# The first RMS norm of a two-model kernel: loads in pieces, squares on two engines, h in tiles of its own

## The reference, cut to what matters

```python
def _rmsnorm(x, g):
    xf = x.astype(jnp.float32)
    y = xf * lax.rsqrt(jnp.mean(xf * xf, axis=-1, keepdims=True) + EPS)
    return (y * g.astype(jnp.float32)).astype(x.dtype)

h = _rmsnorm(x, mix_norm_even[i])                 # x: 512 x 1024
cq, ckv, k_rope, rq, rk, rv, rg = _split(h @ w_in_even[i], EVEN_SPLIT)
...                                               # attention and retention, projection, FFN;
                                                  # then three more layers of other kinds
```

## Time and profile before

| | us |
|---|---|
| median of 3 runs | 2610.37 (2609.48 to 2611.45) |
| profiled execution, whole | 2610.0 |
| its span, first to last instruction | 2608.2 |
| mean granted TensorE clock | 0.948 of full |
| PE busy | 2327.7 (89%) |
| DVE busy / ACT busy / POOL busy | 1249.5 / 1218.0 / 251.7 |

### The profile page before, as it was taken

One profiled execution on the slowest core, in us unless ns is written; L12 is line 12 of the kernel. 1 busy time (PEld: TensorE's weight loads), 2 busy tenths in 40 slices (PEclk: granted clock), 3 DMA queues, 4 the chain that ended last, 5 costly groups with the idle time before them and its releaser, 6 DMA issues.

```text
span 2608.2 us, 29069 instructions
## 1 busy us (share of the span) xinstructions
PE 2327.7 (89%) x11390; PEld 1063.0 (41%) x11390; DVE 1249.5 (48%) x2431; ACT 1218.0 (47%) x2096; POOL 251.7 (10%) x332
## 2 busy tenths in 40 slices
PE   5989998999989888899989899979987899888994
PEld 1434653444434444344434346533323343343332
DVE  3556645456445435575564494543116544543213
ACT  5633555666547445555565664531116563321112
POOL 0000000000001220000000000112220201111131
PEclk8999999999999989999999999979998999888997
DMA  4220002221223200221222221439972220227996
GB/s 172 74 108 8 1 33 89 106 97 67 89 95 118 78 33 33 81 97 65 87 83 106 97 90 52 185 112 383 399 286 99 76 104 16 106 92 267 406 410 252
DMA packets 67753, 335.87 MB, mean 129 GB/s; under 512 B 12008, under 2 KB 12040, under 8 KB 53408
## 3 DMA queue, kind: packets, MB, share of 16 engines
q1 hardware_dynamic: 50448, 266.11, 26.9%
q0 software_dynamic: 17168, 67.90, 6.8%
HBM read 370.64 MB, written 23.07 MB: 151 GB/s over the span
## 4 chain that ended last, share of the span: by engine, by line
PE 64%; DVE 17%; ACT 11%; issue 5%; DMA 2%; POOL 1%; DVEq 0%; SPq 0%; ACTq 0%; POOLq 0%
PE PB L3007 8%; PE PB L375 7%; PE PB L376 7%; PE PB L377 7%; DVE WS L313 4%; PE PB L3031 4%; ACT junk L254 4%; PE PB L1548 2%; PE PB L1550 2%; PE PB L1549 2%; PE PB L2994 1%; PE PB L508 1%; ACT WS L300 1%; DMA T<-moe_x,small 1%; PE PB L789 1%
## 5 line engine op out<-in xcount | busy, mean ns | idle before, releaser
L375 PE MATMUL PB<-AS,WS 128*128 128x512 f16 x1480 | 569.6, 385 | 70.0 <-DVE AS L445 33.5
L376 PE MATMUL PB<-AS,WS 128*128 128x512 f16 x1480 | 569.4, 385 | 0.0
L377 PE MATMUL PB<-AS,WS 128*128 128x512 f16 x1480 | 568.4, 384 | 0.0
L313 DVE SCALAR_TENSOR_TENSOR WS<-raw,sc,WS 128x1024 f16<-128x1024 f32 (+3 forms) x288 | 327.0, 1196 | 103.5 <-ACT WS L300 103.5
L300 ACT ACTIVATE WS<-raw,sc 128x1024 f16<-128x1024 f32 (+3 forms) x288 | 283.9, 1056 | 40.8 <-DVE sc L280 40.8
L254 ACT ACTIVATE junk<-raw 128x1024 f16<-128x1024 f32 (+3 forms) x288 | 280.5, 974 | 8.9
L375 PEld LDWEIGHTS PB<-AS,WS 128*128 128x128 f16 x1480 | 146.0, 99 | 276.6 <-issue 65.2
L3007 PE MATMUL PB<-T 128*64 128x512 f32 x768 | 233.7, 613 | 14.3 <-issue 11.6
L377 PEld LDWEIGHTS PB<-AS,WS 128*128 128x128 f16 x1480 | 146.5, 99 | 180.3 <-issue 10.0
L376 PEld LDWEIGHTS PB<-AS,WS 128*128 128x128 f16 x1480 | 146.0, 99 | 175.6 <-issue 14.3
L289 DVE TENSOR_REDUCE sc<-sc 128x1 f32<-128x4 f32 x72 | 11.3, 157 | 364.0 <-POOL sc L268 364.0
(11 more groups left out here) (580 smaller groups left out, 3392.5 us busy)
## 6 DMA issues: line engine op xcount, KB each, us to landing
T<-in_moe_up SPq DMA_DIRECT2D x26, 2048.0 KB, 10.0
raw<-in_w_up SPq DMA_DIRECT2D x22, 2048.0 KB, 8.0
T<-in_moe_down SPq DMA_DIRECT2D x26, 1024.0 KB, 12.6
raw<-in_w_down SPq DMA_DIRECT2D x16, 1408.0 KB, 6.0
raw<-in_w_in_even SPq DMA_DIRECT2D x9, 2048.0 KB, 8.1
raw<-in_w_in_odd SPq DMA_DIRECT2D x8, 2048.0 KB, 7.8
moe_y<-X SPq DMA_DIRECT2D x32, 512.0 KB, 10.0
WS<-in_moe_up SPq DMA_DIRECT2D x6, 2048.0 KB, 14.7
```

Source lines behind the costliest of these rows:

```text
L313: e.scalar_tensor_tensor(lo[q], raw[q], s, hi[q], MUL, SUB).then_inc(*k.s("dve_split").up("lo", i, q))
L375: e.matmul(bank, wh[:, q, c, :], act.hi[c], start=c == 0, stop=False)
L376: e.matmul(bank, wh[:, q, c, :], act.lo[c], start=False, stop=False)
L377: m = e.matmul(bank, wl[:, q, c, :], act.hi[c], start=False, stop=c == kt - 1)
```

## The change

The loads are cut: `ones` alone, X in two halves, the four quarters of the first weight chunk, then csts without `ones` in two parts, each with a semaphore of its own. The engines no longer wait for all of X and csts at the start; PE waits for cols and `ones`, the others for cols, and what else a step reads is waited for at the step. ACT squares x tiles 0, 2, 4, 6 and DVE tiles 1, 3, 5, 7, into eight tiles of their own; DVE adds them in pairs, and PE sums four tiles in place of eight. The squares of the first weights lie around the reciprocal root, two quarters before and two after. h has eight tiles of its own, four of them are made before the scale of the weights is waited for, and the halves of h and those of the weights are written in an interleaved order. Finally `pe_tile` waits, in chunks of four tiles, for the quarter of its own tile, in all projections and not only in the first.

```diff
-    w.wait_ge(*k.s(f"raw{i % 2}").past(i))
+    w.wait_ge(*(k.s(f"raw{i % 2}").past(i) if i else k.s(f"first{q}").past("w")))
@@ pe_tile
-    w.wait_ge(*k.s("dve_split").past("lo", i, 3))
+    w.wait_ge(*k.s("dve_split").past("lo", i, q if CHUNKS[i][2] - CHUNKS[i][1] == 4 else 3))
@@ setup_sp
-    e.dma_start(k.X[:, :, :], k.ins["xT"].rearrange("(t p) s -> p t s", p=128)).then_inc(*k.s("in_x").dma("x"))
-    e.dma_start(k.csts[:, :], k.ins["csts"]).then_inc(*k.s("in_csts").dma("csts"))
-    sp_load(k, e, w, 0)
+    e.dma_start(k.cst("ones"), k.ins["csts"][:, ones:ones + 128]).then_inc(*k.s("in_ones").dma("ones"))
+    for j in range(2):
+        e.dma_start(k.X[:, 4 * j:4 * j + 4, :], k.ins["xT"][512 * j:512 * j + 512, :].rearrange("(t p) s -> p t s", p=128)).then_inc(
+            *k.s(f"x_half{j}").dma("x"))
+    for q in range(4):
+        e.dma_start(k.quarters(0)[1][q], k.ins[CHUNKS[0][0]][q].rearrange("p k c -> p (k c)")).then_inc(*k.s(f"first{q}").dma("w"))
+    e.dma_start(k.csts[:, 0:ones], k.ins["csts"][:, 0:ones]).then_inc(*k.s("in_csts").dma("left"))
+    e.dma_start(k.csts[:, ones + 128:], k.ins["csts"][:, ones + 128:]).then_inc(*k.s("in_csts").dma("both"))
     sp_load(k, e, w, 1)
@@ setup_act, setup_dve, setup_pool (setup_pe: in_ones in their place)
-    w.wait_ge(*k.s("in_x").past("x"))
-    w.wait_ge(*k.s("in_csts").past("csts"))
@@ even0_pe
-    stat(KT, 7, "norm")
+    for i in range(4):
+        w.wait_ge(*v.past("pair", i))
+        e.matmul(PB[7][:, :], k.cst("ones"), m.sq8[2 * i], start=i == 0, stop=i == 3).then_inc(*p.up("sum", "norm", i))
@@ even0_act
-    squares(k.x, m.tmp, "norm")
-    act_squares(k, e, w, 0)
-    w.wait_ge(*p.past("sum", "norm", KT - 1))
+    for i in range(0, KT, 2):
+        w.wait_ge(*k.s(f"x_half{i // 4}").past("x"))
+        e.activation(m.sq8[i], k.x[i], ACT.Square).then_inc(*a.up("square", "norm", i))
+    act_square(k, e, w, 0, 0)
+    act_square(k, e, w, 0, 1)
+    w.wait_ge(*p.past("sum", "norm", 3))
     act_rstd(k, e, w, m.tmp[2], PB[7][:, :], D, k.col("eps6"), "rstd", "norm", sig=a)
-    act_hi(k, e, w, 0)
-    act_norm(k, e, w, "even0", m.tmp)
+    act_square(k, e, w, 0, 2)
+    act_square(k, e, w, 0, 3)
+    normed(0)
+    normed(1)
+    act_hi_quarter(k, e, w, 0, 0)
+    normed(2)
+    normed(3)
+    act_hi_quarter(k, e, w, 0, 1)
+    for i in range(4, KT):
+        normed(i)
+    act_hi_quarter(k, e, w, 0, 2)
+    act_hi_quarter(k, e, w, 0, 3)
+    w.wait_ge(*k.s("in_csts").past("both"))
@@ even0_dve
+    for i in range(1, KT, 2):
+        w.wait_ge(*k.s(f"x_half{i // 4}").past("x"))
+        e.tensor_tensor(m.sq8[i], k.x[i], k.x[i], MUL).then_inc(*v.up("square", i))
+        w.wait_ge(*v.now())
+        w.wait_ge(*a.past("square", "norm", i - 1))
+        e.tensor_tensor(m.sq8[i - 1], m.sq8[i - 1], m.sq8[i], ADD).then_inc(*v.up("pair", i // 2))
+    dve_gains(k, e, w)
+    w.wait_ge(*a.past("rstd", "norm"))
+    for i in range(4):
+        normed(i)
     dve_scale(k, e, w, 0)
-    dve_lo(k, e, w, 0)
-    dve_norm(k, e, w, "even0", "mix_even", m.tmp)
+    normed_lo(0)
+    normed_lo(1)
+    dve_lo_quarter(k, e, w, 0, 0)
+    normed(4)
+    normed(5)
+    normed_lo(2)
+    normed_lo(3)
+    normed(6)
+    normed(7)
+    dve_lo_quarter(k, e, w, 0, 1)
+    for i in range(4, KT):
+        normed_lo(i)
+    dve_lo_quarter(k, e, w, 0, 2)
+    dve_lo_quarter(k, e, w, 0, 3)
```

More of the change, by code:

```diff
@@ L553, in setup_sp @@
 def setup_sp(k, e, w):
+    ones = CST["ones"][0]
     e.dma_start(k.cols[:, :], k.ins["cols"]).then_inc(*k.s("in_cols").dma("cols"))
-    e.dma_start(k.X[:, :, :], k.ins["xT"].rearrange("(t p) s -> p t s", p=128)).then_inc(*k.s("in_x").dma("x"))
-    e.dma_start(k.csts[:, :], k.ins["csts"]).then_inc(*k.s("in_csts").dma("csts"))
-    sp_load(k, e, w, 0)
+    e.dma_start(k.cst("ones"), k.ins["csts"][:, ones:ones + 128]).then_inc(*k.s("in_ones").dma("ones"))
[6 more added lines that the diff above has]
+    e.dma_start(k.csts[:, ones + 128:], k.ins["csts"][:, ones + 128:]).then_inc(*k.s("in_csts").dma("both"))
     sp_load(k, e, w, 1)
 def setup_act(k, e, w):
-    a = k.s("act_setup")
     e.preload_act_table_set(LN_EXP)
     w.wait_ge(*k.s("in_cols").past("cols"))
-    w.wait_ge(*k.s("in_x").past("x"))
-    w.wait_ge(*k.s("in_csts").past("csts"))
     for i, name in enumerate(("mix_even", "ffn0", "mix_odd", "ffn1")):
@@ L579, in setup_dve, with dve_gains @@
 def setup_dve(k, e, w):
-    v = k.s("dve_setup")
     w.wait_ge(*k.s("in_cols").past("cols"))
-    w.wait_ge(*k.s("in_x").past("x"))
-    w.wait_ge(*k.s("in_csts").past("csts"))
     ln = k.sc[:, 56:62].rearrange("p (a b) -> p a b", b=2)
     w.wait_ge(*k.s("act_junk").past("lnb", 2))
-    e.tensor_tensor(k.sc[:, 52:55], ln[:, :, 0], ln[:, :, 1], ADD).then_inc(*v.up("ln"))
+    e.tensor_tensor(k.sc[:, 52:55], ln[:, :, 0], ln[:, :, 1], ADD).then_inc(*k.s("dve_setup").up("ln"))
+def dve_gains(k, e, w):
     w.wait_ge(*k.s("pool_setup").past("gain"))
-    scale_of(e, w, v, k.sc[:, 56:63], 10, k.sc[:, 64:71], k.sc[:, 72:79], k.sc[:, 80:87], "gain")
+    scale_of(e, w, k.s("dve_setup"), k.sc[:, 56:63], 10, k.sc[:, 64:71], k.sc[:, 72:79], k.sc[:, 80:87], "gain")
 def setup_pool(k, e, w):
     w.wait_ge(*k.s("in_cols").past("cols"))
-    w.wait_ge(*k.s("in_x").past("x"))
-    w.wait_ge(*k.s("in_csts").past("csts"))
     w.wait_ge(*k.s("dve_setup").past("ln"))
@@ L601, in setup_pe @@
     w.wait_ge(*k.s("in_cols").past("cols"))
-    w.wait_ge(*k.s("in_x").past("x"))
-    w.wait_ge(*k.s("in_csts").past("csts"))
+    w.wait_ge(*k.s("in_ones").past("ones"))
 def even0_tiles(k):
@@ L609, in even0_tiles @@
         rq, rk, rv, rg = ([k.t(i) for i in range(a, a + 4)] for a in (0, 4, 8, 12))
+        sq8, h0 = [k.t(8 + i) for i in range(KT)], [k.t(i) for i in range(KT)]
         cq, kro, ckv = [k.t(i) for i in (16, 17, 18)], k.t(19), [k.t(20), k.t(21)]
@@ L875, in squares, with normed @@
             e.activation(tmp[i % 2], x, ACT.Square).then_inc(*a.up("square", what, i))
-    squares(k.x, m.tmp, "norm")
-    act_squares(k, e, w, 0)
-    w.wait_ge(*p.past("sum", "norm", KT - 1))
-    act_rstd(k, e, w, m.tmp[2], PB[7][:, :], D, k.col("eps6"), "rstd", "norm", sig=a)
-    act_hi(k, e, w, 0)
-    act_norm(k, e, w, "even0", m.tmp)
+    def normed(i):
+        w.wait_ge(*k.s("dve_setup").past("gain"))
+        w.wait_ge(*v.past("h", "norm", i))
+        e.activation(k.as_hi[i], m.h0[i], ACT.Identity, scale=k.sc[:, 64:65]).then_inc(*a.up("hi", "norm", i))
+    for i in range(0, KT, 2):
[4 more added lines that the diff above has]
+    w.wait_ge(*p.past("sum", "norm", 3))
+    act_rstd(k, e, w, m.tmp[2], PB[7][:, :], D, k.col("eps6"), "rstd", "norm", sig=a)
+    act_square(k, e, w, 0, 2)
[10 more added lines that the diff above has]
+    act_hi_quarter(k, e, w, 0, 3)
+    w.wait_ge(*k.s("in_csts").past("both"))
     for t in range(4):
@@ L1064, in even0_dve, with normed, normed_lo @@
     act = k.normed_parts("even0", 0)
-    dve_scale(k, e, w, 0)
-    dve_lo(k, e, w, 0)
-    dve_norm(k, e, w, "even0", "mix_even", m.tmp)
+    def normed(i):
+        e.scalar_tensor_tensor(m.h0[i], k.x[i], k.col("mix_even", i), m.tmp[2], MUL, MUL).then_inc(*v.up("h", "norm", i))
+    def normed_lo(i):
+        w.wait_ge(*v.past("h", "norm", i))
+        w.wait_ge(*a.past("hi", "norm", i))
+        e.scalar_tensor_tensor(k.as_lo[i], m.h0[i], k.sc[:, 64:65], k.as_hi[i], MUL, SUB).then_inc(*v.up("lo", "norm", i))
+    for i in range(1, KT, 2):
[8 more added lines that the diff above has]
+        normed(i)
+    dve_scale(k, e, w, 0)
+    normed_lo(0)
[12 more added lines that the diff above has]
+    dve_lo_quarter(k, e, w, 0, 3)
+    w.wait_ge(*k.s("in_csts").past("both"))
     for t in range(8):
```

## The result

| | before | after |
|---|---|---|
| median (runs measured side by side) | 2609.93 (2609.3 to 2611.45, 4) | 2592.51 (2586.87 to 2593.24, 4) |
| ratio, 95% interval | | 0.9928 [0.9911, 0.9945] |
| profiled execution, its span | 2610.0, 2608.2 | 2592.3, 2590.5 |
| mean granted TensorE clock | 0.948 | 0.949 |

The change takes 17.4 us off. The forecast was 2592.6. The total is right to 0.1 us, yet the trace shows only 15.1 of the 17.8 us of gain in the place where the prediction looked for them.

What follows compares the result with a forecast made beforehand. PE is the bound from 48.3, so the gain is its last k-tile of tile 0 starting at 30.4 in place of 48.26. Execution 2610.0 - 17.8 = 2592.2, median 0.4 above: 2592.6; range 2587 to 2598.5.

Steps and rivals of the forecast that it cites:

- half 0 of X lands: Loads at the start: 1.05 MB at 311 to 421 GB/s, 2.5 to 3.4 us before 10.2, plus 0.4: 7.9.
- last pair to the root's start: PE's sum of squares: ends 1.2 us after the last pair at 13.3, so the root starts at 14.5.
- ladder: scale to the last low half of h: DVE behind the weights' scale: 12 norm instructions at 0.70 and two weight quarters at 1.22, 10.8 us, from 19.6 to 30.4.
- tile 4 starts: First projection on PE: tiles 1 to 3 run from 31.1 to 46.6, then tile 4; the stage moves whole.
- rival 3: Loads at the start are served singly, not streamed; last k-tile at 49, total 2611, no change; chance 0.02.
- Rival 4: PE, let in earlier, drops to 1.2 GHz in loops that DVE bounds; two such chunks give 2627; chance 0.03.
- SP issues one load more ahead of it, some 0.4: Loads at the start: one more load issued ahead of half 0 of X delays its landing by some 0.4 us.
- a wait for a load after 11: Named sign that the forecast is wrong: ACT or DVE waiting for a load after 11 us.
- Rival 2: Smaller gain at the start, 11 to 14 us (late pieces, POOL's sum, clock, slower pairs): 2596 to 2600; chance 0.09.
- the central value: POOL's first sum of the gains: no cost taken, since it runs in X's shadow; 1.4 us kept for the range.
- later clock dips falling otherwise, +-1: Forecast's own spread: TensorE clock drops falling elsewhere move the total by +-1 us; runs differ by 2.0.
- rival 1: Finer waits pay in later chunks too: up to 10.4 us more, 2582.2; chance 0.06.

Runs made afterwards that it cites:

- the other kernels of the table: Variants of the changed kernel with edits to waits, ladder order, loads, squares, PE warming or `ones`, and the changed kernel rerun; medians 2588.14 to 2599.18.
- again: The changed kernel itself, unedited, measured once more beside the kernels with ones made on the chip: 2591.01, ratio to before 0.9932.
- ones made: The changed kernel with `ones` written by a DVE memset in place of a load: 2588.14, ratio to before 0.9925.
- the four kernels of the table above: Before (2609.93), changed (2592.51), changed measured again (2591.01), and changed with five extra float32 matmuls warming PE ahead of the sums (2590.21).

## Why the prediction was right, step by step

| step | forecast | measured | off by |
|---|---|---|---|
| half 0 of X lands | 7.9 | 9.2 | +1.3 |
| landing to the last pair | 5.4 | 5.7 | +0.3 |
| last pair to the root's start | 1.2 | 2.5 | +1.3 |
| root's start to the weights' high half | 5.1 | 5.4 | +0.3 |
| ladder: scale to the last low half of h | 10.8 | 10.3 | -0.5 |
| tile 4 starts | 46.6 | 49.4 | +2.8 |

**Right.** The mechanism: what the change is worth is the time by which the last k-tile of tile 0 comes sooner, and everything behind it moved with it. Of its 17.8 us it had 7.3 behind the scale of the weights, and 7.8 were measured there; the other 10.5 were to come from a sooner scale, and that gave 7.3. The ladder was right to 0.5, with 0.68 for each instruction of the norm (2.73 for four) in place of 0.70. The quarters held ACT up by no more than 0.1 (the first landed at 13.45, its square began at 13.48), hidden behind the sum; csts left the chain, and chunk 1 was ready in time. The squares on DVE take 0.69 each, as the nearest row said. The pieces were streamed and not served singly, so rival 3 is out: half 1 landed 3.0 behind half 0, 1.05 MB at some 350 GB/s, and the quarters 1.3 behind one another. The Trainium skill gives its two microseconds for each DMA (DMA: Bandwidth & Descriptors, section "Anatomy of one DMA — SWDGE (gpsimd) path") for loads issued from GpSimd, and no such price for each piece is seen in this queue of loads. (There are nine pieces in place of three loads, not eight.) Rival 4 did not happen: the mean granted clock is 0.949 against 0.948.

**Wrong in size: the landing.** The term "SP issues one load more ahead of it, some 0.4" was mis-sized: that load costs 1.6 to 2.7 us from profile to profile, and only 0.46 of it by its issue. Other terms of the step were too careful: without the small load in front the half lands at 6.5 to 7.0 where the step's arithmetic would give some 7.5. Half 1 was forecast for 10.4 and landed at 12.2, where ACT and DVE waited for it (1.82 and 0.22): one of the signs that the prediction itself had named for being wrong, a wait for a load after 11.

**Wrong in size: the sum.** "PE's last sum ended 1.2 after the last square" was read from a PE that had seven sums done. The change makes the sums start earlier and halves them, and so removes the work that warmed PE. The row from which the price was read had a condition that the change took away. Rival 2 named the start's clock only for the first tile. There it cost nothing: 1.2 GHz until about 30.3, where PE still waited for DVE (0.64 before 31.21).

**POOL.** DVE had the sum of the gains ready at 7.16 and POOL began at 9.68. In the other kernels of the table it began between 7.57 and 11.10. So the delay is real, but it stays hidden behind the root, as the central value had it.

**Why the total was right all the same.** At tile 4 the lead was 15.06, at the end 17.73. The lead over the kernel before (ACT's instructions matched one to one; the time is that of the kernel before, "fine in 0" has the finer waits in chunk 0 only, "no fine" has none):

```
at (us)     100    180    300    1000   1500   2300   2400   end
after      15.06  15.06  15.95  16.51  16.26  16.39  18.40  17.73
fine in 0  15.44  15.44  16.24  16.72  16.46  18.69  18.31  17.86
again      16.22  14.66  15.12  15.20  14.92  17.11  16.72  15.82
ones made  17.98  16.47  17.17  17.56  17.28  20.22  22.80  21.88
no fine     6.34   6.35   6.92   7.07   6.82   9.71  12.18  12.05
```

The two large steps of the first row come where PE runs at half clock in one kernel and not in the other. Before has such a stretch at 265.0 that the changed kernel has not, and a longer one from 2333.5 (34.1 us, against 30.7 from 2317.3):

```profile
265.00:268.40 3.40, 3.40 (x5) 1.51 (x5) 1.38 (x2) 0.22 (x1) 0.00 (x0) 0.51 0.02 5
2333.00:2368.00 35.00, 19.59 (x94) 12.31 (x96) 19.92 (x85) 12.50 (x20) 7.25 (x6) 0.51 0.29 103
```

```profile
2316.00:2351.00 35.00, 19.85 (x102) 12.55 (x103) 20.65 (x86) 12.92 (x20) 7.93 (x6) 0.56 0.29 103
```

In the same 35 us PE passes 102 matmuls at a clock of 0.56 and 94 at 0.51. Ten of the 13 profiles have a stretch of 3.4 us that begins between 90.5 and 100.1 and costs them 1.5 to 1.6 of their lead ("again" and "ones made" between 100 and 180); the first profile of the changed kernel and those of the two runs on the finer waits don't have it. So the prediction's "later clock dips falling otherwise, +-1" was the right thought, sized too small: single runs of one kernel lie some 3 us to either side of its median, and that it is the dips in each of them is argued, not shown. In this pair of profiles the two steps, 0.9 and 2.0, are of the size by which the start fell short, and so a start 2.8 short of the forecast came out at the forecast total. That is luck: nothing in the prediction's sum earned it.

**What stays open.** The lead at 1500 is within 1.8 of that at tile 4 in each of the 13 profiles, and from there to the end each gains another 0.1 to 5.2, 3.1 on average, over the one profile of before. The medians agree in part: they gain 2.1 more than the lead at tile 4 on average (from -1.9, with the squares on ACT alone, to +4.1). The total time at half clock doesn't explain it: 273 us before, 268 in the changed kernel, but 282 without fine waits, which gains the most (5.2). Whether a shift of the work by some 15 us lets the late stretches fall better, or another cause of before's profile is behind it, no run here separates. For the rivals: rival 1 is excluded at its 10 us by the run with fine waits in the first chunk alone, and the period in the second FFN is 24.05 as before (24.04). Rival 2 was half true: the pieces were late and the gain at the start was 15.1, just above its 11 to 14. By that alone the median would have been some 2595.

## What to carry to other kernels

Don't put a small load in front of the one that the first computation needs: make constants on the chip, or load them last, and see who waits for them then. A duration is read with the state of its engine: if the change removes the work ahead of a matmul, its price at a cold PE counts, whatever the clock's record says before its first entry. And a total that fits proves no term of its sum; compare at a point ahead of the later drops of the clock, here the first matmul of tile 4.

## What the runs showed of the hardware

- The column of the granted clock reads 1.00 from the start, while float32 matmuls of 128x512 take 1.06 us. The record has no entry there; its first, at full clock, falls within 0.2 us of the first matmul of 0.59 in the four kernels of the table above.
- With a 64 KB load ahead of it the first 1 MB landed at 8.6 to 9.2 us in eight profiles, without it at 6.5 to 7.0 in four. The share of the DMA engines doesn't set that alone: from 4 to 6 us it was 0.74 in one of the eight and 0.94 in another (9.2 and 9.0).
- POOL's first sum over partitions begins 0.3 to 3.8 us after its operands are there. The latest starts, 10.64 to 11.10, are those of the three kernels that made `ones` on the chip, which give POOL nothing more to do.
- PE was at half clock in a stretch of 3.4 us in which it was busy throughout (265.0, above). Where such stretches fall changes from kernel to kernel, and from one profile of the changed kernel to the other; one of them cost 1.5 to 1.6 us of lead.
